# One attention head in a slot, v rows 36 slots behind u, tile 1's query weights from the single ring, and v rows in rounds of 4 experts of 32 tokens

## What is computed

```python
xn = RMSNorm(x);  z = xn @ w_in                    # q_a k_a v_a q_b k_b v_b g_a g_b
h  = x + (sigmoid(g_a) * (A(xn) @ w_a) + sigmoid(g_b) * (B(xn) @ w_b)) @ w_o
q  = RMSNorm(h) @ w_q                              # 8 heads x 2 halves x 128
top 16 of each half, top 16 of their sums          # 16 experts and 16 gates a head
u = take(u_tab, experts)                           # 128 rows of 1024 per token
act = gelu(sum(hn * u)) ;  v = take(v_tab, experts)
y = h + sum over experts of gate * act * v         # then a last RMSNorm
```

## Time and profile before

| | us |
|---|---|
| median of 3 runs | 2288.86 |
| lowest and highest | 2268.92, 2290.09 |
| the profiled execution's own time | 2268.69 |
| its span | 2266.7 |
| VectorE, GpSimd and TensorE busy | 1203.7, 1165.1, 1539.8 |
| moved by DMA | 688.65 MB, mean 304 GB/s |

### The profile page before, as it was taken

One profiled execution on the slowest core, in us unless ns is written; L12 is line 12 of the kernel. 1 busy time (PEld: TensorE's weight loads), 2 busy tenths in 40 slices (PEclk: granted clock), 3 DMA queues, 4 the chain that ended last, 5 costly groups with the idle time before them and its releaser, 6 DMA issues.

```text
span 2266.7 us, 19117 instructions
## 1 busy us (share of the span) xinstructions
PE 1539.8 (68%) x5562; PEld 719.4 (32%) x5562; DVE 1203.7 (53%) x3269; ACT 365.7 (16%) x897; POOL 1165.1 (51%) x1081
## 2 busy tenths in 40 slices
PE   6999869876688755665665665556556655744567
PEld 4444336554444322222232222223222222211111
DVE  1024440126666654667666776676677666664300
ACT  1002332222222110011111111111111110110000
POOL 2010000003323366677777767677677777776764
PEclk9999978888779877777778788788888778876799
DMA  9989943316545499999999999999999999999997
GB/s 327 369 287 372 349 137 102 131 47 196 194 143 174 135 361 406 345 351 349 362 348 369 355 347 345 337 358 349 359 362 330 346 350 371 337 371 394 346 359 281
DMA packets 207448, 688.65 MB, mean 304 GB/s; under 512 B 20888, under 2 KB 33080, under 8 KB 207320
## 3 DMA queue, kind: packets, MB, share of 16 engines
q0 software_dynamic: 166912, 612.40, 73.7%
q1 hardware_dynamic: 40432, 75.03, 9.5%
HBM read 682.82 MB, written 72.65 MB: 333 GB/s over the span
## 4 chain that ended last, share of the span: by engine, by line
PE 28%; issue 23%; DVE 15%; DMA 14%; POOL 14%; another core or an unknown queue 3%; ACT 2%; SPq 1%; POOLq 1%; DVEq 0%; ACTq 0%
POOL arena L524 8%; DMA XS<-in_peer_u_dram,e_all 7%; DVE XS L1223 6%; PE bank L754 6%; PE bank L871 5%; DMA arena<-in_peer_v_dram,arena 4%; POOL XS L524 4%; PE bank L857 3%; PE bank L957 3%; PE bank L936 3%; POOL PP L524 2%; DMA arena<-in_peer_u_dram,e_all 1%; PE bank L977 1%; DMA WR<-out_dram 1%
## 5 line engine op out<-in xcount | busy, mean ns | idle before, releaser
L857 PE MATMUL bank<-arena 128*64 128x512 f32 x1536 | 661.4, 778 | 288.2 <-DMA arena<-in_peer_v_dram,arena 217.5
L524 POOL DMA_INDIRECT XS<-in_peer_u_dram,e_all x384 | 418.8, 1091 | 585.2 <-DVE e_all L1205 255.0
L1223 DVE SCALAR_TENSOR_TENSOR XS<-XS,GT 128x1024 f32<-128x1024 f32 x384 | 463.2, 1225 | 260.1 <-DMA XS<-in_peer_u_dram,e_all 229.6
L524 POOL DMA_INDIRECT arena<-in_peer_v_dram,arena x384 | 447.9, 1166 | 164.9 <-issue 112.0
L857 PE MATMUL bank<-PP,arena 128*64 128x512 f32 x512 | 331.7, 780 | 250.5 <-DMA arena<-in_peer_v_dram,arena 208.6
L857 PEld LDWEIGHTS bank<-arena 128*64 128x64 f32 x1536 | 175.5, 172 | 630.8 <-issue 629.0
L593 ACT ACTIVATE XS<-bank 128x256 f32<-128x256 f32 (+1 forms) x90 | 36.3, 406 | 1002.4 <-remote 655.0
L857 PEld LDWEIGHTS bank<-PP,arena 128*64 128x64 f32 x512 | 79.7, 174 | 352.0 <-issue 259.0
L871 PE MATMUL bank<-WR,XS 128*128 128x512 f32 x320 | 157.1, 649 | 21.3 <-ACT GT L645 20.1
L1223 DVE SCALAR_TENSOR_TENSOR arena<-arena,GT 128x1024 f32<-128x1024 f32 x128 | 156.6, 1224 | 19.1 <-DMA arena<-in_peer_u_dram,e_all 12.5
L977 PE MATMUL bank<-XS,WR 128*128 128x128 f32 x1024 | 135.7, 291 | 43.5 <-issue 41.6
(11 more groups left out here) (194 smaller groups left out, 1658.5 us busy)
## 6 DMA issues: line engine op xcount, KB each, us to landing
out_dram<-in_cache_a_k_dram POOLq DMA_DIRECT2D x8, 4064.0 KB, 51.2
out_dram<-in_cache_a_v_dram POOLq DMA_DIRECT2D x8, 4064.0 KB, 51.0
WR<-in_w_in_dram SPq DMA_DIRECT2D x8, 2048.0 KB, 22.7
GT<-in_w_peer_q_dram SPq DMA_DIRECT2D x8, 1024.0 KB, 5.6
WR<-in_w_peer_q_dram SPq DMA_DIRECT2D x4, 2048.0 KB, 32.0
XS<-in_peer_u_dram,e_all POOLq DMA_INDIRECT x384
arena<-in_peer_v_dram,arena POOLq DMA_INDIRECT x384
GT<-in_x_prompt_dram SPq DMA_DIRECT2D x8, 512.0 KB
```

What stands on the lines that cost most here:

```text
L524: nc.gpsimd.indirect_dma_start(dst, None, table, bass.IndirectOffsetOnAxis(ap=idx, axis=0))\
L857: last = nc.tensor.matmul(b[c][R * j:R * j + R, :], diag[v // 2 % 2][:, s % 8, :], V[V_AT[s]][:, c * CHUNK:(c + 1) * CHUNK], start=False, ...
L1223: V_.scalar_tensor_tensor(u, u, 1.0, hidden[q // TILE_Q], ALU.mult, ALU.mult, accum_out=dots[:, s // TOPK % 4, s % TOPK:s % TOPK + 1]).the ...
```

## The change

LAG goes from 20 to 36, and an attention head has one slot throughout, so that tile 2's attention begins in slot 32 and tile 3's in 48 (it began in 31 and 39). The slots of tile 2's, SAMPLE's and tile 3's "branches", "merged" and "out" move with it. Since the last "out" is now in slot 70, tile 1's queries (slots 55 to 76) take their weights from `w_q0` as tile 0's do: eight further loads of 1 MB, and `w_q` is loaded after them. G goes from 2 to 4, and R from 64 to 32: a round is one quad, a matmul of v has 32 columns of weights, `regroup` makes 16 copies of 32 partitions by 4 in place of 4 copies of 64 by 8, and the diagonals have half the size. SyncE's queue has the sample tokens' `hn_scratch` before tile 1's answer. `square` of tile 1 uses another scratch place.

```diff
-SLOT0, LAG = 31, 20
+SLOT0, LAG = 31, 36
-G = 2
+G = 4
...
     for i in range(TILES * NH):
-        x = i if i < SLOT0 else SLOT0 + (i - SLOT0) // 2
+        x = i
...
-    put(SLOT0 + 17, "post", TILES - 1)
-    for t, (a, b, c, d, e) in {0: (19, 20, 21, 21, 22), 1: (33, 34, 35, 35, 36), 2: (40, 41, 42, 42, 43),
-                               SAMPLE: (44, 45, 46, 46, 47), 3: (48, 49, 50, 50, 51)}.items():
+    put(SLOT0 + 34, "post", TILES - 1)
+    for t, (a, b, c, d, e) in {0: (19, 20, 21, 21, 22), 1: (33, 34, 35, 35, 36), 2: (50, 51, 52, 52, 53),
+                               SAMPLE: (56, 57, 58, 58, 59), 3: (67, 68, 69, 69, 70)}.items():
...
-            def query_weights(h):
-                if h:
-                    filled(sp, "query", 0, h - 1, 0)
-                sp.dma_start(w_q0, w_pq_v[:, :, 2 * h * P:(2 * h + 2) * P]).then_inc(S["wq0_in"], 16)
+            def query_weights(n):
+                if n:
+                    filled(sp, "query", (n - 1) // PH, (n - 1) % PH, 0)
+                sp.dma_start(w_q0, w_pq_v[:, :, 2 * (n % PH) * P:(2 * (n % PH) + 2) * P]).then_inc(S["wq0_in"], 16)
...
-                        nc.scalar.activation(junk if t else XS[:, 0:D], resid[t], ACT.Square, accum_out=hss).then_inc(S["hstat"], 1)
+                        if t == 1:
+                            filled(act, "query", 0, PH - 1, 0)
+                        nc.scalar.activation(junk if t >= 2 else XS[:, 0:D], resid[t], ACT.Square, accum_out=hss).then_inc(S["hstat"], 1)
...
-                        if t == 0:
-                            pe.wait_ge(S["wq0_in"], 16 * (h + 1))
-                        elif t == 1 and h % 2 == 0:
+                        if t <= 1:
+                            pe.wait_ge(S["wq0_in"], 16 * (PH * t + h + 1))
+                        elif t == 2 and h % 2 == 0:
                             pe.wait_ge(S[f"wq_in{h // 2}"], 16)
...
-                                weights = w_q0[:, k, c * P:(c + 1) * P] if t == 0 else w_q[:, k, (2 * h + c) * P:(2 * h + c + 1) * P]
+                                weights = w_q0[:, k, c * P:(c + 1) * P] if t <= 1 else w_q[:, k, (2 * h + c) * P:(2 * h + c + 1) * P]
```

More of the change, by code:

```diff
@@ L470, in _ @@
             sp.dma_start(gate_a[SAMPLE][0:DEC, :], g_scratch[:, 0:D]).then_inc(S["ga_in"], 16)
-            query_weights(5)
+            for h in range(5, PH + 1):
+                query_weights(h)
             x_again(2)
-            query_weights(6)
             filled(sp, "out", 2, 1, 0)
             sp.dma_start(gate_b[SAMPLE][0:DEC, :], g_scratch[:, D:2 * D]).then_inc(S["gb_in"], 16)
-            query_weights(7)
+            query_weights(PH + 1)
             x_again(SAMPLE)
+            for h in range(2, 5):
+                query_weights(PH + h)
             sp.wait_ge(S["onorm"], 2 * TILES)
@@ L481, in _ @@
             x_again(3)
+            for h in range(5, PH):
+                query_weights(PH + h)
             filled(sp, "out", 3, 1, 0)
@@ L490, in _ @@
             answer(0)
-            answer(1)
             sp.wait_ge(S["hn"], ALL)
             sp.dma_start(hn_scratch, hidden[SAMPLE][0:DEC, :]).then_inc(S["hn_out"], 16)
-            answer(2)
+            answer(1)
             sp.wait_ge(S["hn_out"], 16)
@@ L498, in _ @@
                 sp.dma_start(hbc[b], hn_scratch[b, :].partition_broadcast(P)).then_inc(hb_in[b], 16)
+            answer(2)
             answer(3)
```

## The result

The changed kernel takes 2385.1 us (median; 2368.3 to 2387.3), the kernel before 2278.9 in the same comparison: a ratio of 1.0455 (95%: 1.0364 to 1.0546). It is slower by 4.5%, where 2293 us and no change were forecast and 2350 was the upper end. A second comparison gave 1.0369 (1.0282 to 1.0455). The profiled execution has a span of 2384.3 us, so the sum of the prediction, 2271, is short by 113 us. The stage times of after_out_later in the table further down come from an execution in the slower of that kernel's two states (2365.6 us, the others 2330.2 to 2350.7), so they may be too long.

The account below looks back on a forecast made before the run. VectorE work bounds the stretch beside attention, DMA the later stretches with u and v, then v alone. Span 2266.7 + 87 - 193 + 95 + 9 - 8 + 14 = 2271 us; own time 2273, median forecast 2293, range 2236 to 2350.

Parts of the forecast that it names:

- A's waits: VectorE's idle time beside attention, put at 90 us: 34 for the output projection, 27 for scores, 29 of small gaps.
- B's -8 for a freer TensorE: Where u and v gathers alternate, rounds of four halve TensorE's part of a v quad, so GpSimd waits less: -8 us.
- tile 3's merge: Seven VectorE operations of some 0.69 us leave the stage beside attention: 5 us subtracted from its work.
- C's +14: With v alone, two rounds of four in 8 buffers give a pitch of 6.35 us: 36 x 0.4 = +14 us.
- Stage A: Compute-bound stretch beside attention, before v gathers begin: 292 us of VectorE work plus 90 of waits, 382 us.
- The projection's waits: Beside attention, VectorE's waits for the output projection were to stay at 34 us, since ScalarE's order stays.
- the rival of an unchanged idle share: Beside attention, VectorE stays idle 34% of the time: 445 us, +63, total 2356, halfway 2324; chance 0.18.
- the lag's saving: 16 fewer quads of u and v, 16 more of v alone: -193 and +95 us, a gain of 98 us.
- A's growth: The stage beside attention grows from 295 to 382 us, so v begins at 891 where it was 804: +87 us.
- 16 x 12.07: Where u and v gathers alternate, 94 quads for 110, at 12.07 us each: -193 us.
- the 9 for three loads: Three of eight more query weight loads, 2.9 us each, fall where u and v gathers alternate: +9 us.
- the ring: With v alone, a ring of two rounds binds: pitch 6.7 gives 2306 us, pairs at 1.2 GHz 2367; chance 0.12.

Follow-up runs that it names:

- after_out_later: Changed kernel with both output projections of every row tile one slot later on all engines; ratio 1.0354 to the kernel before.
- lag_only: Kernel before with LAG 36 instead of 20, still two heads in a slot and rounds of two; ratio 1.0151 to the kernel before.
- slots_only: Changed kernel with rounds of two (G = 2), keeping one head in a slot, LAG 36 and the extra weight loads; ratio 1.0224 to the kernel before.
- after_half_u: Changed kernel with VectorE's product of u rows over 512 of 1024 columns for the first 36 quads; ratio 1.0323 to the kernel before.
- after_3_loads_less: Changed kernel without the last three of tile 1's eight query weight loads and TensorE's waits for them; ratio 1.0381 to the kernel before.
- rounds_only: Kernel before with v rows in rounds of four (G = 4) and nothing else of the change; ratio 1.0235 to the kernel before.
- filler5_c: Changed kernel with five extra unused matmuls behind each round of v in the stage with v alone; ratio 1.0359 to the kernel before.
- filler_c: Changed kernel with two extra unused matmuls behind each round of v in the stage with v alone; ratio 1.0432 to the kernel before.

## Why the prediction was wrong

Four terms of the sum failed: A's waits, put at 90 us, were 118; B's -8 for a freer TensorE was +12 in this execution; tile 3's merge, some 12 us, had no term in B; C's +14 was +46.

**Stage A: direction right, two terms too small.** VectorE's work was 298 us for 292. The projection's waits stayed at 33 for 34. But scores took 38.5 us for the 27 that I kept, and rows of u with the small gaps 47 for 29: I assumed that one head in a slot would give the chain of scores slack, and it got none (38.2 before), and I had no term for a u ring of four in plain slots of 8 to 9 us, where the waits for u rows went from 9.8 to 27.4. That is the 34 us. A came out halfway between the forecast and the rival of an unchanged idle share (382 and 445); the idle share was 28%, where they had 24 and 34.

**The gain was smaller than its price from the start.** The prediction booked the lag's saving at 98 us (193 - 95) and A's growth at 87. The growth counted 99 us of VectorE work (it was 104.6) and took 12 us of idle time off. All of the benefit so hung on that -12, a judgement and not a row. lag_only and slots_only agree that it isn't there: 1.5% and 2.2% slower with rounds of two kept; in lag_only idle time grew by 27 us, in the changed kernel by 17. after_half_u shows that less work alone would not have brought the gain either: 75 us less of it, and still 3.2% slower than before.

**B: "16 x 12.07" held, its two small terms did not.** The mean of 12.07 includes a start of 177.5 us. The changed kernel's start took 198.2, of which the 9 for three loads were in the sum (after_3_loads_less gives 4 to 9); the other 12 the trace puts with tile 3's merge, which I had subtracted from A (5 us) and added nowhere. No run leaves the merge alone out. VectorE's waits in the first 14 quads of the changed kernel have it, at branches and projection (2 us before):

```profile
DVE GT L1317 <- remote: 11.5, 1, 11.5
DVE GT L1327 <- PE bank L963: 8.1, 1, 8.1
```

GpSimd waited 27 us for VectorE's use of u rows there, for 10 before. In the later 80 quads I took -8 for a freer TensorE. TensorE was freer, 450 us busy against 563 with rounds of two in the same slots, and GpSimd waited nearly three times as long for buffers. In this execution the 80 quads cost +12 us against before's 11.99, +24 against slots_only; the nine executions with rounds of four in these slots and all copies have a mean of 12.06, which is +6 and +18. The coarser ring costs in B too, with the new slots at least (rounds_only has 12.03 for 11.99 and 12.00, no more than scatter); only for C did I work that out. How much of it ScalarE's copies carry is open.

**C: the right mechanism, at a third of its price.** The cycle was put at 10.0 us plus a round. Measured were 10.7 plus 3.6. The 5.5 us from issue to landing came from a single row: over 30 rounds of C before, the rows of a round's last gather landed 6.0 us after its issue (median; 5.2 to 7.8), and 6.1 in the changed kernel. And I had taken the middle of the two clocks, 6.35, because both occur in the trace before. The changed kernel's TensorE waits before every round of C, 1.4 to 7.3 us, and only 5 of 33 rounds took the 1.9 us of the full clock. 36 x 0.4 = 14 us became 36 x 1.28 = 46; the 34 us of C's miss are this and 2 us of end. Of the rivals the ring came true in place and sign, with a pitch of 6.7 where 7.2 was right.

**What was right.** Four column groups run together: the four starts 0.85 us apart at 1.2 GHz, 0.43 at 2.4. By the Trainium skill ("TensorE: Matmul & The Clock Gate", Part 3, measured speedup), three column tiles give 2.38 times one; here, with four, sixteen records at full clock take 1.93 us (filler5_c, from the first start at 2200.84 to the last end), as long as a round of two with eight, so the trace shows nothing lost from two groups to four; how two stand to one no run here shows. The three loads cost 4 to 9 us for 9, the diagonals took 0.42 us for some 0.4, and TensorE had no wait for query weights in the first 14 quads.

The chances were wrong too. The idle share and the ring stood as rivals of 0.18 and 0.12, each priced as if it came alone, and B's price in rounds of four stood only as a bound in words. All three came, the first of them about halfway, and a range made of single rivals had no room for their sum.

## What to carry to other kernels

When work is moved from a DMA-bound stretch into the slack beside a compute-bound one, compare the mover's own engine time with the DMA time saved before anything else: here 105 us of VectorE for 98 us of DMA, so that a gain could only come from idle time that was there before, and that grew by 17 us, all of it in waits for rows of u. A ring's unit of release is a cost of its own: count how many units the ring holds, and if it is two, put issue, landing (the median of many rows, not one) and the consumer's time at its slower clock into one cycle, in every stage that uses the ring. A mean pitch over a long stretch hides its start; read the first quads apart, since loads and merges that a change shifts gather there.

## What the runs showed that I had not expected

- The mean granted clock says little about a round that is waited for. In filler_c it rose from 0.62 to 0.82 and the awaited round stayed at 1.2 GHz after an idle time of 4.4 us, as about every other round did; with TensorE filled through, 0.97, it ran at 2.4.
- Matmuls of no use shortened a stage: 6.69 us a quad of v against 7.23 and 7.25, with ten more records behind each round. The ratios' intervals (1.0359, and 1.0455 or 1.0369 without them) overlap, so the pitch is the evidence.
- The landing of rows took as long with the DMA engines less full: 6.1 us (median) after a round's last issue in the changed kernel's C, with the engines 84% busy, and 6.0 before, with 97%.
